# A decoder trunk's dense layer: hidden activations turned in squares on VectorE, and the second token tile's turning moved

## The reference, cut to what matters

```
h = layer_norm(ALPHA*h + gmlp_mixer(h))          # norm 1
f = (silu(h @ w_gate) * (h @ w_up)) @ w_down     # dense SwiGLU, hidden width 3584
h = layer_norm(ALPHA*h + f)                      # norm 2
h = h + sigmoid(h @ ple_gate + b) * (p @ ple_proj)
h = layer_norm(ALPHA*h + fox_mixer(h))           # norm 3, layer 1
f = top-2-of-8 expert SwiGLU(h)
h = layer_norm(ALPHA*h + f)                      # norm 4
h = h + sigmoid(h @ ple_gate + b) * (p @ ple_proj)
```

## Time and profile before

| | |
|---|---|
| median of 3 runs | 1523.0 us (1522.2 to 1523.5) |
| the profiled execution | 1521.48 us |
| its span, first to last instruction | 1519.7 us |
| TensorE busy | 1476.3 us, 97% |
| VectorE busy | 701.8 us, 46% |
| ScalarE busy | 327.4 us, 22% |
| GpSimd busy | 42.0 us, 3% |
| mean granted TensorE clock | 0.989 of full speed |

### The profile page before, as it was taken

The page is one execution under the profiler, slowest core; times in us unless marked ns, Lnnn a source line. Parts: engine busy times, 40 slices in busy tenths (PEclk is TensorE's granted clock), DMA queues, the critical chain, the costliest instruction groups (busy, mean ns, idle before and its releaser), DMA issues.

```text
span 1519.7 us, 33431 instructions
## 1 busy us (share of the span) xinstructions
PE 1476.3 (97%) x14993; PEld 1029.4 (68%) x14993; DVE 701.8 (46%) x1581; ACT 327.4 (22%) x466; POOL 42.0 (3%) x50
## 2 busy tenths in 40 slices
PE   7999899999899998999999999999999999999987
PEld 6888788888678877767666555555555555556665
DVE  5785665555774677323233232323233232323356
ACT  4543344443345554000000000000000000000022
POOL 2010100000100000000000000000000000000020
PEclk9999999999999999999999999999999999999998
DMA  9866445555345335999999999999999999999960
GB/s 372 308 230 213 145 166 196 210 173 193 136 150 197 112 100 223 391 390 411 410 410 406 409 411 402 411 410 406 411 406 410 402 411 405 411 406 409 404 236 28
DMA packets 196094, 468.46 MB, mean 308 GB/s; under 512 B 7741, under 2 KB 8433, under 8 KB 195441
## 3 DMA queue, kind: packets, MB, share of 16 engines
q1 hardware_dynamic: 191392, 450.92, 77.8%
q0 software_dynamic: 2992, 12.70, 2.2%
q10 hardware_dynamic: 1568, 2.75, 0.5%
HBM read 462.53 MB, written 3.81 MB: 307 GB/s over the span
## 4 chain that ended last, share of the span: by engine, by line
PE 92%; DVE 5%; ACT 1%; DMA 1%; issue 1%; DVEq 0%; ACTq 0%
PE ps L1543 90%; PE ps L1560 1%; DVE acc L1001 1%; DVE stats L1010 0%; DMA ws_raw<-in_gm_w_s_dram 0%; DVE htl L973 0%; ACT split L613 0%; PE ps L1763 0%; DVE h L1006 0%; DVE split L958 0%; PE ps L1860 0%; PE ps L1896 0%; ACT hth L628 0%; DVE m_bt L1485 0%; ACT prob L803 0%
## 5 line engine op out<-in xcount | busy, mean ns | idle before, releaser
L1543 PE MATMUL ps<-ring,xt 128*32 128x256 f32 (+1 forms) x8064 | 625.9, 451 | 1.1 <-DVE m_hb L1477 1.1
L1543 PEld LDWEIGHTS ps<-ring,xt 128*32 128x32 f32 x8064 | 360.7, 109 | 226.3 <-DVE m_hb L1477 1.6
L1543 PE MATMUL ps<-split,hth 128*128 128x512 f32 x1184 | 374.3, 398 | 8.7 <-DVE htl L973 4.5
L1543 PE MATMUL ps<-ring,m_bt 128*32 128x256 f32 (+1 forms) x4032 | 335.8, 451 | 0.6 <-DVE m_bt L1485 0.6
L1473 DVE TENSOR_TENSOR m_hb<-ps,m_sg 128x256 f32<-128x256 f32 x56 | 23.8, 425 | 567.0 <-ACT m_sg L896 556.3
L1543 PEld LDWEIGHTS ps<-split,hth 128*128 128x128 f32 x1184 | 223.6, 191 | 56.0 <-DVE htl L973 7.8
L1543 PEld LDWEIGHTS ps<-ring,m_bt 128*32 128x32 f32 x4032 | 183.4, 109 | 112.7 <-DVE m_bt L1485 1.0
L1485 DVE STREAM_TRANSPOSE m_bt<-m_hb 32x96 f32<-32x96 f32 x896 | 241.4, 269 | 13.1
L1543 PE MATMUL ps<-split,htl 128*128 128x512 f32 x592 | 233.5, 394 | 0.0
L896 ACT ACTIVATE m_sg<-ps 128x256 f32<-128x256 f32 x56 | 21.6, 387 | 788.2 <-PE ps L1543 788.2
L958 DVE TENSOR_TENSOR split<-raw,split 128x2048 fp32r<-128x2048 f32 x50 | 114.0, 2291 | 77.7 <-ACT split L613 77.6
(11 more groups left out here) (234 smaller groups left out, 661.1 us busy)
## 6 DMA issues: line engine op xcount, KB each, us to landing
ring<-in_moe_w_gate_dram SPq DMA_DIRECT2D x112, 1024.0 KB, 11.7
ring<-in_moe_w_up_dram SPq DMA_DIRECT2D x112, 1024.0 KB, 12.7
ring<-in_moe_w_down_dram SPq DMA_DIRECT2D x112, 1024.0 KB, 11.7
raw<-in_gm_w_in_dram SPq DMA_DIRECT2D x14, 1024.0 KB, 13.3
raw<-in_ffn_w_gate_dram SPq DMA_DIRECT2D x14, 1024.0 KB, 5.0
raw<-in_ffn_w_up_dram SPq DMA_DIRECT2D x14, 1024.0 KB, 6.0
raw<-in_ffn_w_down_dram SPq DMA_DIRECT2D x14, 1024.0 KB, 4.9
raw<-in_fox_w_in_dram SPq DMA_DIRECT2D x12, 1024.0 KB, 5.0
```

Of the source, the lines that this page charges most:

```text
L1543: return nc.tensor.matmul(o, a, b, start=start, stop=stop)
```

## The change

It has four parts.

1. In the dense layer's loop VectorE turns `hb` itself into a new SBUF buffer `turned_hb` (in memory that `pp0` uses later), with 16 instructions of 32x256, as two groups of 8 between the remainders. ScalarE's copies of the two PSUM banks become one copy of `turned_hb`, VectorE's two subtractions one. TensorE's 8 transposes go. The last block, behind the loop, stays on TensorE.
2. `cols_by_tile` calls `between` behind tile 0's second half.
3. At norm 2 `turn_tile(1)` becomes such a `between`.
4. `meanwhile` is called behind tile 1's variance, ahead of its centring. At norm 2 the remainder of G_PLE+1 moves there from GpSimd, ahead of G_PLE+2's; ScalarE rounds G_PLE+2 ahead of the square root of tile 1.

```diff
+    turned_hb, _ = at("turned_hb", [P, 4, S], F32, nxt)
     pp0, nxt = at("pp0", [P, T, D], F32, nxt)
 # GpSimd
         pool.dma_start(pn0[:, :, :], p[0, 0].rearrange("(m p) n -> p m n", p=P)).then_inc(pn_landed[0], 16)
-        rest_lo(G_PLE + 1)
 # ScalarE, dense loop
             silu(j)
-            for m in range(T):
-                act.wait_ge(s0["tp"], j * T + (n_tp - T + m + 1))
-                nc.scalar.copy(bth[:, :, m * P:(m + 1) * P],
-                               ps[6 + m][:, :].rearrange("p (c t) -> p c t", t=P)).then_inc(s0["tp_hi"], 1)
+            act.wait_ge(hb_turned, j)
+            act.wait_ge(s0["used"], gj)
+            nc.scalar.copy(bth[:, :, :], turned_hb[:, :, :]).then_inc(hb_hi, 1)
 # ScalarE, norm 2
         round_hi(G_PLE + 1)
+        round_hi(G_PLE + 2)
         norm_sqrt(2, 1)
-        round_hi(G_PLE + 2)
 # VectorE, norm
                     .then_inc(streams[which]["var"], 1)
+                if m == T - 1 and meanwhile is not None:
+                    meanwhile()
...
-            if meanwhile is not None:
-                meanwhile()
             for q in range(2):
                 stream_lo(q, T - 1, which)
 # VectorE, dense loop
+        def turn_rows(q):
+
+            rows = slice(q * G3, (q + 1) * G3)
+            blocks = hb[rows, :, :].rearrange("p m (c s n) -> p m c s n", s=4, n=G3)
+            for s in range(4):
+                to = turned_hb[s * G3:(s + 1) * G3, :, :].rearrange("p c (m t) -> p m c t", m=T)
+                last = nc.vector.transpose(to[:, :, :, rows], blocks[:, :, :, s, :])
+            return last
+
         with dve.Fori(1, NJ) as j:
             gj = dve.snap(g + 4 + (j - 1) * G_BLK)
             rest_at(gj + 1, g + 5)
+            dve.wait_ge(hid_ready, j * T)
+            turn_rows(0)
+            turn_rows(1)
             rest_at(gj + 2, g + 6)
+            turn_rows(2)
+            turn_rows(3).then_inc(hb_turned, 1)
             rest_at(gj + 3, g + 7)
-            for m in range(T):
-                dve.wait_ge(s0["tp_hi"], j * T + (n_tp - T + m + 1))
-                nc.vector.tensor_tensor(btl[:, :, m * P:(m + 1) * P],
-                                        ps[6 + m][:, :].rearrange("p (c t) -> p c t", t=P),
-                                        bth[:, :, m * P:(m + 1) * P].bitcast(F32), ALU.subtract)\
-                    .then_inc(s0["tp_lo"], 1)
+            dve.wait_ge(hb_hi, j)
+            nc.vector.tensor_tensor(btl[:, :, :], turned_hb[:, :, :], bth[:, :, :].bitcast(F32), ALU.subtract)\
+                .then_inc(hb_lo, 1)
             rest_at(gj + 4, g + 8)
             rest_at(gj + 5, g + 9)
             dve.wait_ge(silu_done, j * T + T)
             dve.wait_ge(s0["used"], gj + 4)
+            dve.wait_ge(hb_turned, j)
             hid(j)
 # VectorE, norm 2
         def gate_rest():
-            dve.wait_ge(s0["lo"], G_PLE + 2)
+            rest_lo(G_PLE + 1)
             rest_lo(G_PLE + 2)
 # TensorE, cols_by_tile
-                    if m == 0 and half == 0 and between is not None:
+                    if m == 0 and half == 1 and between is not None:
                         between()
 # TensorE, dense loop
             cols_granules(gj, [0, 1], g_of=g + 4)
-            pe.wait_ge(s0["tp_lo"], j * T + (n_tp - T))
-            for m in range(T):
-                pe.wait_ge(hid_ready, (j - 1) * T + (m + 1))
-                for c in range(4):
-                    last = nc.tensor.transpose(ps[6 + m][:, c * P:(c + 1) * P], hb[:, m, c * P:(c + 1) * P],
-                                               ident[:, :])
-                last.then_inc(s0["tp"], 1)
+            pe.wait_ge(hid_ready, j * T)
             cols_granules(gj + 2, [2, 3], g_of=g + 6)
-            pe.wait_ge(s0["tp_lo"], j * T + n_tp)
+            pe.wait_ge(hb_lo, j)
             down(gj + 4, g + 8, (j - 1) * (2 * T))
 # TensorE, behind norm 2
         rows_granule(G_PLE, pth, ptl, 0, True, True, banks=(4, 5, 0, 1))
-        turn_tile(1)
-        ple(0, G_PLE + 1, fresh)
+        pe.wait_ge(part_added, (NJ - 1) * 2 * T + 3)
+        ple(0, G_PLE + 1, fresh, lambda: turn_tile(1))
```

More of the change, by code:

```diff
@@ L281, in build_trunk @@
     hid_ready = sem("hid_ready")
+    hb_turned = sem("hb_turned")
+    hb_hi = sem("hb_hi")
+    hb_lo = sem("hb_lo")
     part_full = sem("part_full")
@@ L709, in _ @@
             tp_hi(pth[:, :, m * P:(m + 1) * P], 2 * P)
-        n_tp = nt[0]
         with act.Fori(1, NJ) as j:
@@ L723, in _ @@
             silu(j)
-            for m in range(T):
-                act.wait_ge(s0["tp"], j * T + (n_tp - T + m + 1))
-                nc.scalar.copy(bth[:, :, m * P:(m + 1) * P],
-                               ps[6 + m][:, :].rearrange("p (c t) -> p c t", t=P)).then_inc(s0["tp_hi"], 1)
+            act.wait_ge(hb_turned, j)
+            act.wait_ge(s0["used"], gj)
+            nc.scalar.copy(bth[:, :, :], turned_hb[:, :, :]).then_inc(hb_hi, 1)
             for k in range(4, 7):
                 rnd(k)
-        nt[0] += (NJ - 1) * T
         for m in range(T):
@@ L1758, in _ @@
             cols_granules(gj, [0, 1], g_of=g + 4)
-            pe.wait_ge(s0["tp_lo"], j * T + (n_tp - T))
-            for m in range(T):
-                pe.wait_ge(hid_ready, (j - 1) * T + (m + 1))
-                for c in range(4):
-                    last = nc.tensor.transpose(ps[6 + m][:, c * P:(c + 1) * P], hb[:, m, c * P:(c + 1) * P],
-                                               ident[:, :])
-                last.then_inc(s0["tp"], 1)
+            pe.wait_ge(hid_ready, j * T)
             cols_granules(gj + 2, [2, 3], g_of=g + 6)
-            pe.wait_ge(s0["tp_lo"], j * T + n_tp)
+            pe.wait_ge(hb_lo, j)
             down(gj + 4, g + 8, (j - 1) * (2 * T))
-        nt[0] += (NJ - 1) * T
-        assert nt[0] % 2 == 0
         pe.wait_ge(hid_ready, NJ * T)
```

## The result

The changed kernel takes 1511.22 us (median of 4 runs, 1510.51 to 1513.2); the kernel before took 1523.22 on the same chip. The medians differ by 12.0 us; the ratio of the runs is 0.9928 [0.9917, 0.9939], which is 0.7% or 11 us. The profiled execution's own time is 1510.51 us with a span of 1508.8, against 1521.48 and 1519.7 before: 11.0 us less. The forecast was 1509.4, and 1507.9 for the profiled execution. So the difference was smaller than forecast by 2.6 us in the profiled executions (13.6 against 11.0), and the median came 1.8 us above its forecast.

The account below looks back on a forecast made before the run. TensorE's matmul queue was taken to bound the kernel. Terms 5.1 + 2.7 + 5.6 + 0.25 = 13.6 us bring 1521.48 to 1507.9, with 1.5 for the median 1509.4 us; own range 1507.5 to 1511, overall 1506.5 to 1517.

Parts of the forecast that it names:

- rival D: Norms give less: norm 1's other 12 products stay at the lower clock, total 1511 to 1512.5 us; chance 0.15.
- A (dearer): Loop: transposes start every 0.50 to 0.56 us, stalling 2.4 to 8 us in all, 1512 to 1517.5; chance 0.13.
- B (620 ns): Loop: transposes cost 2.2 ns an element, 15 us stall in six iterations, about 1524 us, no change; chance 0.04.
- C (by the square, 720 ns): Loop: transposes cost by the square, a start every 0.73 us, 11 us slower, 1534; chance 0.06.
- The loop, 5.1 forecast: Dense loop: TensorE loses 8 transposes, 0.87 us an iteration, 5.2 in six; 0.1 charged for the first iteration: -5.1 us.
- TensorE wants: Loop: t = 0 is the last down product's end; last remainders due at 21.8, done at 21.4, 0.4 us slack.
- "wrong" sign: Would refute: TensorE idle in the loop over 0.9 us an iteration, or norms' tile 1 products starting no earlier.
- Norm 1, 2.7 forecast: First norm: TensorE runs 24 products before turning the second tile, products end at 186.5 instead of 189.24: -2.7 us.
- Norm 2, 5.6 forecast: Second norm: TensorE runs 24 products instead of waiting; tile 1's end at 425.4, before at 430.95: -5.6 us.
- two things that the prediction named: Second norm: GpSimd's remainder goes, so 3.36 us of VectorE stall vanish; TensorE no longer waits for tile 1's h.
- Norm 4, 0.25 forecast: Last norm: with tile 1 turned behind 24 products, the last product ends at 1514.25 instead of 1514.50: -0.25 us.
- 12 more 2.72: Last norm: the second twelve products, moved ahead of the turn, take 2.72 us, at full speed.

Follow-up runs that it names:

- e1: Kernel before with part 1 alone (VectorE turns `hb` in the dense loop), norms as before; 1518.08 us, ratio 0.9972.
- e3: Kernel before with norm 2's change alone (moved remainders, tile 1 turned behind tile 0's products); 1518.17 us, ratio 0.9972.
- e2: Kernel before with only tile 1 turned behind both halves of tile 0 at norms 1 and 4; 1522.43 us, ratio 0.9995.
- e10: e9 with one strip of `hb` (4 transposes) turned one iteration early in the dense loop; 1509.34 us, ratio 0.9914.
- e6: Changed kernel with four more 32x256 transposes an iteration on VectorE, one strip turned twice; 1522.23 us, ratio 0.9998.
- e4: Kernel before with norm 2's change except TensorE's order: remainders moved on VectorE, tile 1 still turned ahead of all products; 1524.88 us, ratio 1.0010.
- e0: The changed kernel run and profiled again, nothing altered; 1512.25 us, ratio 0.9930.
- e7: Changed kernel with the first two strips of `hb` turned one iteration earlier, between the down sums; 1516.04 us, ratio 0.9956.
- e5: Changed kernel with norm 4 alone back in the old order; 1511.42 us, ratio 0.9923.
- e9: Changed kernel with tile 1's turn split at norms 1 and 2, G_FFN+2 rounded ahead of acc copies, norm 4 in old order; 1510.29 us, ratio 0.9919.
- e8: e7 plus tile 1's turn split in halves at norms 1, 2 and 4, and G_FFN+2 rounded ahead of acc copies; 1511.68 us, ratio 0.9928.

## Why the prediction was right, and where its terms were off

The forecast, faster by the removal of TensorE's own work, holds: e1 and e3 each give 0.28% alone, and the sum of the single parts e1, e2 and e3 (9.3 us by their ratios, 10.1 by their medians) agrees with the 11 to 12 of the whole within their intervals. Three of four terms were 0.4 to 0.8 us too large, and the smallest had the wrong sign; together they make 3.0 us (13.6 against 10.6), while the median missed the forecast by 1.8. That it came so near has a part of luck: the forecast set the median 1.5 us above the profiled execution, as it was before, and this time it was 0.7 above it. The median of 1511.22 is also just outside the forecast's own range of 1507.5 to 1511, and inside that of rival D (1511 to 1512.5), though D's condition did not come at norm 1, whose part gave 2.3 us and not 0 to 1.

**The transpose.** Forecast 438 ns and a start every 0.45 us, worked out from a fixed part and 1.046 ns an element; measured 436 ns and 0.45. A (dearer), B (620 ns) and C (by the square, 720 ns) are out as to the price; the wait for the remainder by which A would have shown itself came all the same, small, for another reason (below).

**The loop, 5.1 forecast, 4.3 measured.** The forecast had VectorE finish at t = 21.4; in the trace the last remainder ends at 242.02, t = 21.54, 0.14 late against the forecast. The larger error is in the deadline. (The 21.8 us are the 96 products of gate and up; the down product of a block is 48, two granules of 24, and not 96 as the description of the kernel has it.) The prediction set "TensorE wants" at the time when the products before are complete (21.8). TensorE takes the next granule's first weight load ahead of that: at 21.34 where nothing holds it (e10). So the slack was not 0.4 us but -0.2, and the same holds for the third remainder (0.17 at 236.53). The waits come to 2.4 us by the loads over the whole stage; the products feel less, 0.11 to 0.16 us an iteration (32.80 against 32.69 before and 32.64 in e10), about 0.9 us in all by the stage (197.06 against 6 x 32.69), of which the forecast had charged 0.1. The "wrong" sign the prediction had named, idle over 0.9 us an iteration, did not come; but e6 shows how near it was, since every further transpose costs its whole length.

**Norm 1, 2.7 forecast, 2.3 measured.** The second twelve products did run at the full clock from about 165: 24 are over at 168.02, forecast 167.9. The turn and its idle (0.96) were as forecast. The wait for the remainder of G_FFN+2 was 0.3, forecast 0.4: the last product ahead of it starts at 175.22, the next at 175.71. What was missing is a price for the break itself. The forecast counted 0.227 us a product. A run of products that follows other work of TensorE keeps to that (84 in 19.10, 0.03 over), but one that follows an idle wait takes 0.3 more: 48 in 11.18 against 10.90, 72 at norm 4 in 16.63 against 16.34. By the timelines 0.12 of it is in the first three products (175.71 to 176.51 where 0.68 would do), and the rest is overlap that is lost at a break: a product is listed with 0.39 us and the next one starts 0.227 behind it, but behind a wait none is under way. The change makes one or two such breaks at each norm, since the turn there has nothing over it.

**Norm 2, 5.6 forecast, 4.9 measured (5.0 in e3).** The steps came in the forecast's order: remainders 403.67, centring pair 1.53, 24 products, the turn, no half clock. Measured against the forecast, each moved by the 6.6 us gained up to there: the first product at 406.10 for 406.0, the end of the 24 at 411.80 for 411.46, the end of the 48 at 424.83 for 424.2. It is again the breaks: one ahead of the 24 products, one ahead of the 48. Of the two things that the prediction named, the vanished stall paid nothing in e4, where TensorE still waited for tile 1's h. The 3.36 us of stall were real (4.89 against 1.53), but 4.4 us of remainders took their place ahead of tile 1's h, one from GpSimd and one that VectorE had made behind h; the prediction had h 1.0 later, and e4's wait is 1.02 longer. The gain needs TensorE's order. How much of it the order would give with the remainders in their old places is open (see e4).

**Norm 4, 0.25 forecast, -0.9 measured.** The failed step is "12 more 2.72", full speed for the second twelve. The prediction took the moment when the clock had risen, 4.7 us after the restart, from the earlier trace rows as if it were fixed. In the changed kernel it rose later: between 1480 and 1485 us the granted clock is 0.76, and the 24 products take 8.45 us, where the forecast had 7.62 (4.90 and 2.72). That is 0.8 of the 1.1 us; 0.3 is the break before the 72 products, as above. It was no single late rise: with 24 products in a row e2, e0, e7 and e6 take 8.54, 8.25, 8.22 and 8.18 us. It was the profiled execution of the kernel before that was early. With the old order all of the twelve products are slow in e3, e4, e5 and e9; only in e1, in e10 and in the profile that the forecast was read from is the last of them fast. The forecast rested on one execution. In the old order a late rise costs nothing: the slow time lies under the wait for tile 1's h, 5.6 us after the restart (1488.46 to 1494.08), where slow and fast products are equally in time. That is rival D's mechanism, at the place where the prediction had not looked for it. e5 shows it by undoing it: there the twelve products are slow to the last, and the stage is 40.01 us all the same.

## What to carry to other kernels

When a filled engine stands before a deadline of TensorE's, measure the deadline from the start of its first weight load for the new operand in a trace where nothing holds it, not from the end of the products before; the 0.4 us between them was the whole slack here. Work that fills the wait of an engine that has just restarted is worth nothing while the clock is low, if the wait hid the low clock already: at norm 4 the same reordering that gave 2.3 us at norm 1, and 4.9 at norm 2 together with the moved remainders, lost 0.9. And when a stall is removed by moving work, count all the work that comes onto the stalled engine's path with it: at norm 2 a stall of 3.36 us went and 4.4 us came, and this paid only because TensorE no longer waited there.

## What the runs showed of the hardware

- VectorE's transpose of f32 in 32x32 squares: 32x96 takes 270 ns and 32x256 takes 436 ns, so 1.04 ns an element and 170 ns fixed (two sizes only). Eight in a row take 3.57 us, so they do not overlap. The Trainium skill, "VectorE: DVE Perf Modes", section on the TRN2 errata, states 58 fixed cycles in its table and about 150 as measured; 170 ns is 163 cycles at the 0.96 GHz it gives, and this trace agrees with the second figure.
- After an idle stretch TensorE's products took 0.43 us each and later 0.23. The moment of the change differed between executions: at norm 4 the first product listed with 0.39 us started 4.7 us after the restart before, 6.1 in e2 and 6.0 in the changed kernel, with the same twelve products ahead.
- Spans of the same changed kernel were 1508.8 and 1510.5 us in two profiles. The 1.7 us between them are all there by the restart at norm 1 (160.65 against 162.31), and the granted clock from 10 to 20 us is 1.00 in one and 0.83 in the other. Why an execution gets the one or the other is open.
- The same wait of TensorE of 2.0 us in the middle of products was followed by a lower clock in one execution (e7: 0.66 from 195 to 200 us, 1.6 us lost beside the wait) and not in another (e8: 1.00). The waits of 0.96 and 0.90 us behind the turns at norms 1 and 2 of the changed kernel were followed by products of full speed.
- TensorE's first weight load for a new operand started at 242.55 in e10, 0.22 us before the first product that uses it (242.77), while the products before were still under way (the last one from 242.55 on).
- VectorE's centring pair beside a running GpSimd remainder took 4.89 us, and 1.53 without it, in the changed kernel and in e4 alike.
